# Issuing layer 1's context experts in pieces between the phases of layer 2 that read only latent tokens

## The chip, the cores and the metric

The kernel runs as one program on one core of a Trainium2 chip. The metric is the device time of that program in microseconds (us), lower is better. The kernel before takes 5995.83 us, the median of three runs (5993.45 to 5997.48).

## The reference

Two layers of one block run over 512 latent tokens and 256 context tokens, width 1024. Everything is float32. Per layer, cut to what matters here:

```python
mod_lat = cond_lat @ w_mod[l] + b_mod[l]          # and mod_ctx, from another condition
h  = rmsnorm(x) * (1 + sc1) + sh1;  hc = the same of ctx
p  = h @ w_in[l]                                   # q, k, v | short conv | hyena | gates
kvc = hc @ w_in[l][:, K0:SC0]                      # all the last layer needs of the context
y_att = attend(q, [kc, k], [vc, v])                # latent queries see context keys and values
y_sc, y_hy = short_conv(...), hyena(...)           # hyena: FFT convolutions with generated filters
x = x + gt1 * merge(gates, y_att, y_sc, y_hy)      # and ctx likewise, in layer 1 only
h2 = rmsnorm(x) * (1 + sc2) + sh2                  # and h2c
f = peer(h2 and h2c): per token and each of 8 heads
      s1, s2 = top16 of 128 scores each; top16 of their 256 sums -> 16 expert numbers e, softmax g
      a = gelu(u_tab[e] . h2);  f = sum(g * a * v_tab[e])
x = x + gt2 * f[latent];  ctx = ctx + gt2c * f[context]
```

Two layers run. The context is updated in layer 1 and read in layer 2 by the keys and values of attention alone, so everything of layer 2 that comes from x alone, up to attention, needs no context experts.

## The kernel before, in words

Tokens lie in tiles of 128 on the partitions: 4 latent tiles (NT_LAT), 2 context tiles. The program is a chain of phases. A `Phase` is a block with one instruction stream for each engine; all engines meet at its end. No scheduler orders anything: each engine runs its stream as written and waits on semaphores.

Per layer the phases are: `phase_mod` (24 blocks of w_mod of 1 MB, each split into a rounded high part and a low part, products on TensorE; the filter network's angles on GpSimd), `phase_norm1`, `phase_qkv`, `phase_attention`, `phase_conv_branches` (24 column blocks of w_in, each 24 matmuls per 512 tokens), then `phase_spectrum` and `phase_long_conv` for each of two orders (and for each length, 512 and 256, in layer 1), `phase_merge`, `phase_out`, `phase_norm2`, `phase_query`, `phase_experts`.

`SplitRing` feeds the weight blocks: SyncE loads block n into slot n % slots once the job that used the slot is done, ScalarE rounds it (L296), GpSimd subtracts (L262), TensorE uses it. In `phase_conv_branches` the ring has 4 slots.

`phase_experts` (L1686) is a loop over tiles (6 in layer 1, 4 in layer 2), heads (8) and 16 experts per head. One expert of one head and tile is one item; 768 items in layer 1, of which 256 are of the context. For an item GpSimd issues an indirect DMA of one row of 8 KB (u and v) for each of 128 tokens into one of 8 slots (L1733); VectorE forms the dot product (L1837); ScalarE takes Gelu (L1767); VectorE scales an identity by it (L1845); TensorE multiplies that diagonal by the v half, two float32 matmuls of 512 columns that the profile shows as four rows (L1749). The slot is then free. Between the items of a head VectorE finds the next head's 16 experts in five parts.

Of the kernel before, what the change touches and what calls it, by code (L numbers as in the profile page):

```python
# [138 lines left out]
class Phase:  # L139
# [4 lines left out]
    def __init__(self, nc):  # L144
        self.nc, self.sems = nc, []
        Phase.count += 1
        self.tag = f"p{Phase.count}"
# [6 lines left out]
    def __enter__(self):  # L154
        self.stack = ExitStack()
        self.block = self.stack.enter_context(self.nc.Block())
        return self
# [8 lines left out]
class Chip:  # L166


    def __init__(self, nc, ctx, io):
        self.nc, self.io = nc, io  # L170
        self.arena_at, self.views = (nc.sbuf_base + 31) // 32 * 32, {}
        self.arena = ctx.enter_context(nc.sbuf_tensor("arena", [P, 201 * 256], F32))
# [160 lines left out]
def filter_hidden(c):  # L333

    return c.at(107, T_ALL)


class FilterMlp:


    def __init__(self, c, ph, layer, width):
        self.c, self.layer, self.width = c, layer, width
        self.z, self.h1, self.h2 = c.at(160, T_ALL), c.at(163, T_ALL), filter_hidden(c)
        self.a, self.r = c.at(166, 2, T_ALL), c.at(172, T_ALL)
        self.w1, self.w2 = c.at(176, FH), c.at(176.25, FH)
# [3 lines left out]
    def sync(self, sp):  # L349
        io, layer = self.c.io, self.layer  # L350
        sp.dma_start(self.z[0:EMB, :], io["feat"]).then_inc(self.landed, 16)
# [16 lines left out]
    def vector(self, dve, i):  # L368
# [4 lines left out]
        c.nc.vector.tensor_scalar(self.a[0:FH, i, 0:self.width], c.psum[0:FH, at:at + self.width], c.cols[0:FH, b:b + 1],  # L373
                                  c.cols[0:FH, b + 1:b + 2], ALU.add, ALU.mult).then_inc(self.shifted, 1)

    def gpsimd(self, pool):

        nc, st = self.c.nc, Steps(pool, self.steps)
        r, w = self.r[0:FH, 0:self.width], slice(0, self.width)
        for i in range(2):  # L380
            a, part = self.a[0:FH, i, w], self.z[0:FH, w]
            pool.wait_ge(self.shifted, i + 1)
            if i:
                pool.wait_ge(self.sined, 1)
            st.do(nc.gpsimd.tensor_scalar(r, a, 1.0 / TWO_PI, ROUND, ALU.mult, ALU.add))
            st.wait()
            st.do(nc.gpsimd.tensor_scalar(r, r, ROUND, None, ALU.subtract))
            st.wait()
            for piece in (PI_HI, PI_MID, PI_LO):
                st.do(nc.gpsimd.tensor_scalar(part, r, piece, None, ALU.mult))  # L390
                st.wait()
                st.do(nc.gpsimd.tensor_tensor(a, a, part, ALU.subtract))
                st.wait()
            nc.gpsimd.tensor_scalar(r, a, PI_F32, -PI_F32, ALU.min, ALU.max).then_inc(self.reduced, 1)

    def scalar(self, act, i):
        act.wait_ge(self.reduced, i + 1)
        self.c.nc.scalar.activation((self.h1, self.h2)[i][0:FH, 0:self.width], self.r[0:FH, 0:self.width],
                                    ACT.Sin).then_inc(self.sined, 1)


def phase_mod(c, layer, full):
# [18 lines left out]
    with Phase(nc) as ph:  # L421
# [4 lines left out]
        mlp = FilterMlp(c, ph, layer, T_ALL if full else L_LAT)  # L426
# [17 lines left out]
        def _(act):  # L444
# [6 lines left out]
            for n in range(2 * chunks):  # L451
# [17 lines left out]
                if n in (12, 23):  # L469
                    mlp.scalar(act, n // 23)  # L470
# [3 lines left out]
        def _(pool):  # L474
            mlp.gpsimd(pool)
# [31 lines left out]
        def _(dve):  # L507
# [21 lines left out]
            for t in range(NT):  # L529
# [3 lines left out]
                c.mod[:], c.psum[:, 7 * 512:7 * 512 + 2 * N_MOD].rearrange("p (j s) -> p j s", s=2),  # L533
                c.cols[:, C_BMOD:C_BMOD + N_MOD].unsqueeze(2).to_broadcast([P, N_MOD, 2]), ALU.add))
# [96 lines left out]
def phase_qkv(c, layer, full):  # L631

    nc, io = c.nc, c.io
    qT, kT, vN = c.at(116, PAIRS, T_ALL), c.at(128, KV_HEADS, T_ALL), c.at(134, NT, P)
    sqb = c.at(143, 2, 640)
    qn = c.at(148, 2, 640)
    qr = c.at(153, 2, 640)
    kd = c.at(158, 2, 256)
    tmp = c.at(160, 4, 320)
    gain = c.at(166, 640)  # L640
    w = c.rounded(72, 6, KD, P), c.rounded(48, 6, KD, P)
    ssq = c.at(169, 2, 16)
    rr = c.at(169.5, 2, 16)
    tiles = list(range(NT))
    with Phase(nc) as ph:
# [14 lines left out]
        def _(pe):  # L660
            def project(t):
# [4 lines left out]
                pairs = products((c.hT_high, c.hT_low), w)  # L666
# [582 lines left out]
def phase_long_conv(c, length, order):  # L1249

    nc = c.nc
# [743 lines left out]
```

## Time and profile before

| | us |
|---|---|
| median of 3 runs | 5995.83 |
| profiled execution, span from first to last instruction | 6004.9 |
| layer 1's expert loop, 6 tiles | 2105.0 |
| layer 2's expert loop, 4 tiles | 1412.0 |
| layer 2, from the end of layer 1's loop to the start of `phase_merge` | 661.5 |

The profiled execution and the runs without a profile differ by 0.2%. A row of the profile's page gives an engine's busy time in the span; a stretch of time (a "window") can be asked for its busy times, TensorE's granted clock (1.00 is 2.4 GHz, 0.50 is 1.2 GHz) and the share of time in which the 16 DMA engines were busy. The two expert loops take 59% of the span. TensorE is busy 78% of the span, VectorE 62%, ScalarE 21%, GpSimd 32%, and 1342 of 1503 MB are moved by the gathers.

### The profile page before, as it was taken

The numbers are of one execution on the slowest core, as the hardware profiler recorded it, in microseconds if no ns is written. First come the engines' busy times: TensorE is split into PE (matmuls) and PEld (weight loads), VectorE is DVE, ScalarE is ACT, GpSimd is POOL, SyncE is SP. The second block draws the span as 40 slices with busy tenths as digits, with TensorE's granted clock in tenths as the row PEclk, the third lists the DMA queues.
The fourth block names the chain that finished last, engine by engine and source line by source line (L and its number), as shares of the span: only waits on it lengthen the run. The fifth ranks groups of instructions, "written<-read, shape, count | busy, mean of one in ns | idle before, by whom it ended". The sixth has DMA issues, their size and how long they took to land. (4 is left out here: it accounts for less than half of the span.)

```text
span 6004.9 us, 54671 instructions
## 1 busy us (share of the span) xinstructions
PE 4691.4 (78%) x14264; PEld 2532.4 (42%) x14264; DVE 3701.3 (62%) x8357; ACT 1237.8 (21%) x2616; POOL 1943.0 (32%) x1532
## 2 busy tenths in 40 slices
PE   6999879977777777777777777998977777777776
PEld 3567348855232323222333325563864223233322
DVE  6422451343777778777877876234234778778777
ACT  5322012212111111111111134320322111111111
POOL 4012002222443434444343432120432333444443
PEclk8899989979898889888888887999988889888888
DMA  5011002204999999999999981020314999999998
GB/s 215 15 35 68 4 26 64 67 28 168 386 394 383 384 385 396 383 380 397 378 387 379 400 356 43 28 74 7 98 69 195 380 394 381 385 382 396 381 384 343
DMA packets 223038, 1503.36 MB, mean 250 GB/s; under 512 B 25284, under 2 KB 25668, under 8 KB 51852
## 3 DMA queue, kind: packets, MB, share of 16 engines
q0 software_dynamic: 184320, 1342.26, 55.2%
q1 hardware_dynamic: 38412, 157.98, 7.3%
q8 instruction: 75, 1.23, 0.1%
q14 instruction: 231, 1.89, 0.1%
HBM read 1498.04 MB, written 2.10 MB: 250 GB/s over the span
## 5 line engine op out<-in xcount | busy, mean ns | idle before, releaser
L1749 PE MATMUL psum<-arena 128*128 128x512 f32 x5120 | 2554.1, 656 | 960.4 <-DVE arena L1845 955.3
L1733 POOL DMA_INDIRECT arena<-in_uv,arena x1280 | 1415.0, 1105 | 2072.4 <-PE psum L1749 1715.3
L1749 PEld LDWEIGHTS psum<-arena 128*128 128x128 f32 x5120 | 1040.9, 210 | 2472.8 <-DVE arena L1845 1368.8
L1837 DVE SCALAR_TENSOR_TENSOR arena<-arena 128x1024 f32<-128x1024 f32 x1280 | 1555.3, 1220 | 254.1 <-issue 194.1
L947 PE MATMUL psum<-view_at,view_at 128*128 128x512 f32 (+1 forms) x4896 | 949.6, 356 | 19.2 <-issue 9.7
L262 POOL TENSOR_TENSOR view_at<-view_at,view_at 128x1024 fp32r<-128x1024 f32 (+1 forms) x184 | 396.5, 2166 | 1490.3 <-ACT view_at L296 1489.0
L947 PEld LDWEIGHTS psum<-view_at,view_at 128*128 128x128 f32 x4896 | 812.8, 190 | 153.1 <-issue 21.7
L1767 ACT ACTIVATE arena<-arena 128x1 f32<-128x1 f32 x1280 | 252.2, 202 | 2932.7 <-DVE arena L1837 2930.6
L1845 DVE TENSOR_SCALAR arena<-ident,arena 128x128 f32<-128x128 f32 x1280 | 451.3, 353 | 57.4 <-ACT arena L1767 49.2
L1482 DVE TENSOR_TENSOR view_at<-view_at,psum 128x768 f32<-128x768 f32 (+1 forms) x48 | 39.4, 821 | 372.0 <-PE psum L947 372.0
L1871 DVE TENSOR_TENSOR arena<-psum,arena 128x1024 f32<-128x1024 f32 x80 | 98.0, 1225 | 267.8 <-PE psum L1749 267.8
L262 DVE TENSOR_TENSOR view_at<-view_at,view_at 128x2048 fp32r<-128x2048 f32 (+5 forms) x122 | 200.5, 1670 | 72.9 <-ACT view_at L455 44.0
L296 ACT ACTIVATE view_at<-view_at 128x1024 fp32r<-128x1024 f32 (+1 forms) x172 | 159.6, 938 | 386.5 <-DMA view_at<-in_w_in 255.5
L874 DVE TENSOR_REDUCE arena<-psum 128x1 f32<-128x768 f32 (+1 forms) x80 | 68.1, 851 | 172.8 <-PE psum L834 172.2
L1767 ACT ACT_TABLE_LOAD x120 | 154.0, 1283 | 11.3 <-issue 9.8
L495 PE MATMUL psum<-view_at,cond 128*4 128x512 f32 x384 | 108.7, 424 | 48.3 <-ACT view_at L455 25.1
L1532 PE MATMUL psum<-view_at,view_at 128*128 128x512 f32 x480 | 115.4, 403 | 30.8 <-POOL view_at L262 17.3
L1191 PE MATMUL psum<-arena 128*128 128x512 f32 x288 | 126.2, 594 | 4.2 <-DVE arena L1229 4.2
L670 PE MATMUL psum<-view_at,view_at 128*128 128x256 f32 (+1 forms) x528 | 97.9, 349 | 29.4 <-PEq L163 29.4
L1796 DVE COPY arena<-arena 128x256 f32 (+1 forms) x82 | 23.5, 286 | 157.5 <-POOL arena L1721 157.5
L1532 PEld LDWEIGHTS psum<-view_at,view_at 128*128 128x128 f32 x480 | 93.7, 196 | 52.1 <-issue 29.6
L1790 DVE MAX8 arena<-arena 128x8 f32<-128x128 f32 (+1 forms) x246 | 83.5, 339 | 37.6 <-DVE arena L1788 36.1
(187 smaller groups left out, 3778.5 us busy)
## 6 DMA issues: line engine op xcount, KB each, us to landing
view_at<-in_w_in SPq DMA_DIRECT2D x108, 512.0 KB, 5.1
view_at<-in_w_mod SPq DMA_DIRECT2D x48, 1024.0 KB, 11.3
arena<-in_uv,arena POOLq DMA_INDIRECT x1280
view_at<-in_w_br SPq DMA_DIRECT2D x48, 256.0 KB
arena<-in_dft SPq DMA_DIRECT2D x2, 4096.0 KB
view_at<-in_w_out SPq DMA_DIRECT2D x16, 512.0 KB, 8.6
view_at<-in_wq SPq DMA_DIRECT2D x16, 512.0 KB
arena<-in_x SPq DMA_DIRECT2D x1, 2048.0 KB
```

What stands on the lines that cost most here:

```text
L262: return eng.tensor_tensor(lo, x, hi.bitcast(F32), ALU.subtract)
L296: self._high(act, lambda out, x: self.c.nc.scalar.activation(out, x, ACT.Copy), n)
L495: last = nc.tensor.matmul(c.bank(q % 2, 512, 4), c.cond4[:, half * HALF + k], part[:, n % 2, k * 512:(k + 1) * 512], start=(half == 0 and ...
L947: last = nc.tensor.matmul(c.psum[:, bank * 512 + lo:bank * 512 + hi], a[:, k], b[:, k, lo:hi], start=(k == 0 and i == 0), stop=(k == kt - ...
L1191: last = nc.tensor.matmul(out, table, hw[:, t, src * W_BR:(src + 1) * W_BR], start=(i == 0), stop=(i == nt - 1))
L1532: last = nc.tensor.matmul(c.bank(2 * (t % 4) + h), a[:, k, t * P:(t + 1) * P], b[:, 4 * h:4 * h + 4, k, :], start=(k == 0 and i == 0), sto ...
L1733: nc.gpsimd.indirect_dma_start(out=slots[k % RING], out_offset=None, in_=table, in_offset=bass.IndirectOffsetOnAxis(ap=eidx[:, p, k:k + 1] ...
L1749: last = nc.tensor.matmul(c.bank(2 * p + h), diag[:, k % 4], slots[k % RING][:, D + h * 512:D + (h + 1) * 512], start=(k == 0), stop=(k == ...
L1767: nc.scalar.activation(gelus[:, p, k:k + 1], dots[:, p, k:k + 1], ACT.Gelu).then_inc(gelued, 1)
L1837: nc.vector.scalar_tensor_tensor(out=junk[:, k % 2], in0=slots[k % RING][:, 0:D], scalar=1.0, in1=h2N[:, bass.ds(t, 1)].rearrange("p a n - ...
L1845: nc.vector.tensor_scalar(diag[:, k % 4], c.ident[:], gelus[:, p, k:k + 1], probs[:, p, k:k + 1], ALU.mult, ALU.mult).then_inc(diag_ready, 1)
L1871: nc.vector.tensor_tensor(upd, c.psum[:, 1024 * p:1024 * p + D], gate2[:, bass.ds(t // NT_LAT, 1)].rearrange("p a n -> p (a n)"), ALU.mult ...
```

## The change

Layer 1's `phase_experts` now runs over the 4 latent tiles only. The 256 items of the context are written out without a loop by a class `CtxExperts`, whose four methods issue the items of one engine up to a given number. A `Share` tells a phase how many items stand behind each of its steps. Layer 2 starts with `context_beside`: modulation (24 steps, 48 items), latent spectra (13 steps and 40 items each), norm of the latent tokens (9 steps, 12), convolution projections (24 steps, 88), the two long convolutions (7 steps, 12; 9 steps, 16). Behind them stand a norm phase for the context alone, then qkv, attention, merge as before.

An item differs in this: 6 slots for gathers and not 8, Gelu and the diagonal both on ScalarE (three instructions L495, L499, L504 of the new kernel), the sums of all 8 heads of a tile stay in one pair of PSUM banks. Each engine issues the items up to another bound: GpSimd 3 ahead of the step's number, VectorE to it, ScalarE 1 and TensorE 2 behind it.

```diff
+class CtxExperts:
+    RING, SUM_LAG, FETCH = 6, 2, 3
+    def gather(self, pool, n):
+        for i in range(self.n_gathered, self.up_to(n, self.FETCH)):
+            if i >= self.RING:
+                pool.wait_ge(self.slot_used, i - self.RING + 1)
+            nc.gpsimd.indirect_dma_start(...)
+    def weigh(self, act, n):
+        for i in range(self.n_weighed, self.up_to(n, -1)):
+            act.wait_ge(self.dotted, i + 1)
+            nc.scalar.activation(gelus, dots, ACT.Gelu)
+            nc.scalar.activation(scaled, gelus, ACT.Copy, scale=probs)
+            if i >= 4:
+                act.wait_ge(self.slot_used, i - 3)
+            nc.scalar.activation(self.diag[:, i % 4], self.c.ident[:], ACT.Copy, scale=scaled)
+    def sum_up(self, pe, n):
+        for i in range(self.n_summed, self.up_to(n, -self.SUM_LAG)):
+            pe.wait_ge(self.diag_ready, i + 1)
+            for h in range(2): nc.tensor.matmul(self.c.bank(6 + h), ...)
+    def dot(self, dve, n):
+        for i in range(self.n_dotted, n):
+            dve.wait_ge(self.landed[i % self.RING], 16 * (i // self.RING + 1))
+            nc.vector.scalar_tensor_tensor(out=self.junk, in0=slot, in1=h2N, accum_out=dots)
+class Share:
+    def place(self, s):
+        return self.first + self.n * (s + 1) // self.steps
+def phase_mod_beside(c, layer, lay, share):   # as phase_mod, 3 slots, low parts by DVE (even) and GpSimd (odd)
+            for n in range(n_all):             # GpSimd's stream
+                if n % 2:
+                    split(nc, nc.gpsimd, high, low, raw)
+                next(angles, None)             # one piece of the filter's angles
+                share.gpsimd(pool, n)
 def phase_conv_branches(...):
-        ring = SplitRing(c, ph, conv_blocks(c, layer), ahead=4)
+        ring = SplitRing(c, ph, conv_blocks(c, layer), at=lay.ring_at, slots=lay.ring_slots, ahead=lay.ahead)
...   # in layer 2 ring_slots = ahead = 3
+            for n in range(len(jobs)):         # GpSimd's stream
+                if n + lay.ring_slots < len(jobs):
+                    ring.split(pool, blocks=(n + lay.ring_slots,))
+                share.gpsimd(pool, n)
                 feature_job(c, ring.parts(n), ...).then_inc(proj, 1)      # TensorE's stream
...
+                share.tensor(pe, n)
                 ring.round_ahead(act, n, proj)                            # ScalarE's stream
...
+                share.scalar(act, n)
+                share.vector(dve, n)                                      # VectorE's stream
+def context_beside(c, layer, lay):
+    phase_mod_beside(c, nxt, lay, Share(experts, 0, 48, 24))
+    for order in range(2):
+        phase_spectrum(c, nxt, L_LAT, order, lay, Share(experts, 48 + 40 * order, 88 + 40 * order, 13), spectra[order])
+    phase_norm1_apart(c, range(NT_LAT), ..., Share(experts, 128, 140, KD + 1), [(keep_x, x_lat)])
+    phase_conv_branches(c, nxt, lay, Share(experts, 140, 228, 24), [(keep_ysc, lay.ysc)])
+    for order, (first, last) in enumerate(((228, 240), (240, 256))):
+        phase_long_conv(c, L_LAT, order, lay, Share(experts, first, last, 7 + 2 * order), loads of the kept spectra)
+    phase_norm1_apart(c, range(NT_LAT, NT), ..., Share(), [(x_lat, keep_x), (lay.ys[1], keep_ysc)])
```

Since the gather slots and the context's scores hold memory that layer 2 used, the latent x, the short convolution's result and both spectra are stored to HBM and loaded back. The blocks of phases with items close without GpSimd's drain.

ScalarE's stream in layer 2's `phase_conv_branches` before: L1054 evacuates a job's product, L296 rounds weight blocks, L1059 prepares the convolution.

```order
L1054 ACTIVATE arena<-psum 128x512
L296 ACTIVATE view_at_1527<-view_at_1525 128x1024
L1059 ACTIVATE arena<-arena,cols 128x512
L296 ACTIVATE view_at_1527<-view_at_1525 128x1024 x2
L1054 ACTIVATE arena<-psum 128x512
L296 ACTIVATE view_at_1527<-view_at_1525 128x1024
```

The same place now: L1570 and L1575 are the old L1054 and L1059, L297 the rounding, L495, L499 and L504 an item's Gelu, weight and diagonal, L486 the softmax of the next head.

```order
L1570 ACTIVATE arena<-psum 128x512
L297 ACTIVATE view_at_14342<-view_at_14340 128x1024
L495 ACTIVATE arena<-arena 128x1
L499 ACTIVATE arena<-arena 128x1
L504 ACTIVATE arena<-ident,arena 128x128
L495 ACTIVATE arena<-arena 128x1
L499 ACTIVATE arena<-arena 128x1
L504 ACTIVATE arena<-ident,arena 128x128
L486 ACT_TABLE_LOAD
L486 ACTIVATE arena<-arena 128x16
L495 ACT_TABLE_LOAD
```

The items of a step stand behind the rounding of the block that comes three jobs later.

GpSimd's stream in the same phase before: L262 makes the low parts, L997 restores h at the end.

```order
L999 UNCONDITIONAL_BRANCH
L262 TENSOR_TENSOR view_at_1526<-view_at_1525,view_at_1527 128x1024 x20
L997 TENSOR_TENSOR view_at_49<-view_at_50,view_at_51 128x768 x3
```

The same place now: L263 is the old L262 and L475 the gather of an item.

```order
L1509 UNCONDITIONAL_BRANCH
L263 TENSOR_TENSOR view_at_14341<-view_at_14340,view_at_14342 128x1024
L475 DMA arena<-in_uv,arena 128x2048 x3
L263 TENSOR_TENSOR view_at_14341<-view_at_14340,view_at_14342 128x1024
L475 DMA arena<-in_uv,arena 128x2048 x4
L263 TENSOR_TENSOR view_at_14341<-view_at_14340,view_at_14342 128x1024
L475 DMA arena<-in_uv,arena 128x2048 x4
```

The three or four gathers of a step stand behind the low part of the block three jobs later, and the restoring of h is gone in layer 2.

GpSimd's stream in layer 2's modulation now (before it held only the filter's angles): L697 to L707 are pieces of these angles.

```order
L907 UNCONDITIONAL_BRANCH
L475 DMA arena<-in_uv,arena 128x2048 x5
L263 TENSOR_TENSOR view_at_10729<-view_at_10726,view_at_10732 128x2048
L475 DMA arena<-in_uv,arena 128x2048 x4
L263 TENSOR_TENSOR view_at_10728<-view_at_10725,view_at_10731 128x2048
L697 TENSOR_SCALAR arena<-arena 64x512
L475 DMA arena<-in_uv,arena 128x2048 x2
L700 TENSOR_SCALAR arena<-arena 64x512
L475 DMA arena<-in_uv,arena 128x2048 x2
```

Between every second pair of gathers GpSimd now makes the low part of a block of 2048 columns, which VectorE made before.

## Rows read from the trace of the kernel before

**Rows 1.** The page: span and busy time of each engine.

```profile
span 6004.9 us, 54671 instructions
PE 4691.4 (78%) x14264; PEld 2532.4 (42%) x14264; DVE 3701.3 (62%) x8357; ACT 1237.8 (21%) x2616; POOL 1943.0 (32%) x1532
```

**Rows 2.** Windows of the two expert loops, layer 1 then layer 2.

```profile
core 0: us, PE busy (x) PEld busy (x) DVE busy (x) ACT busy (x) POOL busy (x), PEclk, DMA share, GB/s
1434.40:3539.40 2105.00, 1530.59 (x3072) 624.73 (x3072) 1659.69 (x4262) 326.15 (x987) 849.72 (x769) 0.87 0.95 383
4577.50:5989.50 1412.00, 1023.53 (x2048) 416.20 (x2048) 1112.90 (x2854) 218.04 (x659) 565.57 (x513) 0.87 0.94 381
```

**Rows 3.** Groups of instructions in layer 1's loop, by line.

```profile
L1749 PE MATMUL psum<-arena 128*128 128x512 f32 x3072 | 1530.6, 655 | 573.1 <-DVE arena L1845 569.6
L1837 DVE SCALAR_TENSOR_TENSOR arena<-arena 128x1024 f32<-128x1024 f32 x768 | 933.1, 1220 | 149.0 <-issue 112.8 <-DMA arena<-in_uv,arena 33.3
L1733 POOL DMA_INDIRECT arena<-in_uv,arena x768 | 849.6, 1106 | 1240.3 <-PE psum L1749 1023.1 <-issue 154.2 <-DVE arena L1824 63.1
L1767 ACT ACTIVATE arena<-arena 128x1 f32<-128x1 f32 x768 | 151.3, 202 | 1757.4 <-DVE arena L1837 1756.9
L1767 ACT ACT_TABLE_LOAD x72 | 92.4, 1283 | 6.8 <-issue 6.0
```

**Rows 4.** Timeline of TensorE in layer 1's loop, around one idle time.

```profile
2399.68 5.31 PE L1749 MATMUL psum<-arena 128*128 128x512 f32 x12
...
2415.03 10.89 PE L1749 MATMUL psum<-arena 128*128 128x512 f32 x20 [10.04 <-DVE arena L1845]
```

**Rows 5.** Windows of layer 2's phases: modulation, norm, conv branches, (spectrum, long conv) twice.

```profile
3539.40:3627.30 87.90, 65.54 (x292) 25.86 (x292) 65.12 (x41) 62.41 (x54) 46.47 (x18) 0.92 0.71 289
3627.30:3656.50 29.20, 8.61 (x48) 7.22 (x48) 25.74 (x34) 13.71 (x22) 10.26 (x4) 0.62 0.29 109
3856.30:4000.50 144.20, 134.81 (x608) 111.22 (x608) 36.68 (x45) 42.20 (x56) 54.04 (x23) 0.98 0.23 73
4000.50:4059.40 58.90, 55.35 (x118) 22.97 (x118) 20.75 (x24) 7.41 (x9) 0.00 (x0) 0.86 0.22 81
4059.40:4100.50 41.10, 30.80 (x72) 13.55 (x72) 22.17 (x34) 1.19 (x2) 0.00 (x0) 0.96 0.00 0
4100.50:4159.10 58.60, 53.74 (x118) 21.78 (x118) 20.74 (x24) 7.41 (x9) 0.00 (x0) 0.88 0.04 9
4159.10:4200.60 41.50, 32.15 (x104) 21.15 (x104) 22.88 (x42) 1.54 (x4) 0.00 (x0) 0.92 0.00 1
sum 461.40, PE 380.99 PEld 223.75 DVE 214.07 ACT 135.88 POOL 110.77; mean PE 54.43 PEld 31.96 DVE 30.58 ACT 19.41 POOL 15.82
```

**Rows 6.** Timeline of layer 2's conv branches: jobs, then one block's way.

```profile
3904.62 30.76 PE L947 MATMUL psum<-view_at,view_at 128*128 128x512 f32 x135
...
3933.38 0.78 ACT L1070 ACTIVATE arena<-psum,cols 128x512 f32<-128x512 f32 x1 [0.86 <-PE psum L947]
...
3936.96 1.06 ACT L296 ACTIVATE view_at<-view_at 128x1024 fp32r<-128x1024 f32 x1 [2.80 <-DMA view_at<-in_w_in]
3937.92 0.40 ACT L1044 ACTIVATE arena<-arena 128x256 f32<-128x256 f32 x1
3938.10 2.40 POOL L262 TENSOR_TENSOR view_at<-view_at,view_at 128x1024 fp32r<-128x1024 f32 x1 [3.11 <-ACT view_at L296]
```

**Rows 7.** Groups in layer 2's modulation: the split by VectorE, the rounding, the angles.

```profile
L262 DVE TENSOR_TENSOR view_at<-view_at,view_at 128x2048 fp32r<-128x2048 f32 x24 | 58.0, 2429 | 21.4 <-ACT view_at L455 21.3
L455 ACT ACTIVATE view_at<-view_at 128x2048 fp32r<-128x2048 f32 x24 | 45.8, 1908 | 28.4 <-DMA view_at<-in_w_mod 14.4 <-PE psum L495 13.9
L390 POOL TENSOR_SCALAR arena<-arena 64x512 f32<-64x512 f32 x6 | 18.7, 3111 | 0.5
L385 POOL TENSOR_SCALAR arena<-arena 64x512 f32<-64x512 f32 x2 | 1.2, 616 | 47.7 <-DVE arena L373 47.7
```

**Rows 8.** Timeline of layer 2's norm: a subtraction on VectorE alone, then beside GpSimd's.

```profile
3630.36 0.69 DVE L262 TENSOR_TENSOR view_at<-view_at,view_at 128x512 fp32r<-128x512 f32 x1 [0.24 <-ACT view_at L600]
...
3633.58 5.11 POOL L262 TENSOR_TENSOR view_at<-view_at,view_at 128x1024 fp32r<-128x1024 f32 x2 [13.57 <-ACT view_at L296]
3634.05 2.43 DVE L262 TENSOR_TENSOR view_at<-view_at,view_at 128x512 fp32r<-128x512 f32 x1 [1.50 <-ACT view_at L600]
```

More of the change, by code:

```diff
@@ L386, in gpsimd @@
             st.wait()
-            st.do(nc.gpsimd.tensor_scalar(r, r, ROUND, None, ALU.subtract))
+            yield
+            st.do(nc.gpsimd.tensor_tensor(a, a, part, ALU.subtract))
             st.wait()
[L389 to L394, printed above, removed]
@@ L474, in _ @@
         def _(pool):
-            mlp.gpsimd(pool)
+            for i in range(2):
+                for _ in mlp.gpsimd(pool, i):
+                    pass
         @ph.block.tensor
@@ L811, in phase_attention @@
             "values_summed", "y_kept", "dve_steps"))
-        ring = SplitRing(c, ph, conv_blocks(c, layer)[:4])
+        ring = SplitRing(c, ph, conv_blocks(c, layer)[:0 if lay.apart else lay.ahead])
         @ph.block.sync
@@ L992, in _ @@
             ring.load(sp, proj)
+            if stores:
+                sp.wait_ge(sc_done, KB_BR)
+                for dst, src in stores:
+                    sp.dma_start(dst, src).then_inc(stored, 16)
+                sp.wait_ge(stored, 16 * len(stores))
         def restore(eng, ks):
@@ L1000, in _ @@
         def _(pool):
-            ring.split(pool)
-            pool.wait_ge(proj, len(jobs))
-            restore(nc.gpsimd, range(5, KD))
+            ring.split(pool, blocks=range(lay.ahead, lay.ring_slots))
+            for n in range(len(jobs)):
+                if n + lay.ring_slots < len(jobs):
+                    ring.split(pool, blocks=(n + lay.ring_slots,))
+                share.gpsimd(pool, n)
+            if not lay.apart:
+                pool.wait_ge(proj, len(jobs))
+                restore(nc.gpsimd, range(5, KD))
         @ph.block.tensor
@@ L1115, in dft_views, with phase_spectrum @@
         at += tiles * w / 256
-    out["all"] = c.at(48, int((at - 48) * 256))
+    out["all"] = c.at(first, int((at - first) * 256))
     return out
-def spectrum_views(c, nt):
-    return c.at(152, nt, W_BR), c.at(160, nt, W_BR), c.at(168, W_BR)
 def spectrum_jobs(nt):
     return [(w, f) for f in range(nt) for w in ("re", "im")] + [("top", 0)]
-def phase_spectrum(c, layer, length, order):
+def phase_spectrum(c, layer, length, order, lay, share, keep=None):
     nc, io = c.nc, c.io
@@ L1154, in _ @@
             if order == 0:
-                sp.dma_start(tab["all"], io[f"dft{length}"]).then_inc(tab_in, 16)
+                sp.dma_start(*lay.filter_tables(io, length)).then_inc(tab_in, 16)
+            if keep is not None:
+                for n, (what, ft) in enumerate(jobs):
+                    sp.wait_ge(kept, n + 1)
+                    src, to = {"re": (kre[:, ft], ft), "im": (kim[:, ft], nt + ft), "top": (kre_b, 2 * nt)}[what]
+                    sp.dma_start(keep[:, to], src).then_inc(stored, 16)
+                sp.wait_ge(stored, 16 * len(jobs))
         @ph.block.tensor
@@ L1206, in _ @@
                 nc.scalar.activation(ab[t % 2], hw[:, t], ACT.Abs).then_inc(ab_d, 1)
+                share.scalar(act, t)
+            for n in range(len(jobs)):
+                share.scalar(act, nt + n)
+        @ph.block.gpsimd
+        def _(pool):
+            for n in range(nt + len(jobs)):
+                share.gpsimd(pool, n)
         @ph.block.vector
```

732 lines of the change are left out of this document (602 added, 130 removed).

## The prediction

> **What bounds the kernel now.** I read the page first, then windows of both expert loops and of layer 2's phases, then the groups by line inside them, and last timelines where a wait decides. The page gives the weights: TensorE is busy 78% of 6004.9 us, VectorE 62%, ScalarE 21% [rows 1]. The windows say that two regimes alternate. In an expert loop the DMA engines are busy 94 to 95% at 381 to 383 GB/s while TensorE is idle 27% of the time [rows 2]. Layer 1's loop takes 2105.0 / 768 = 2.741 us for an item, and its 1.049 MB at 383 GB/s take 2.738 us, so the transfer alone fills the time. In the phases the reverse holds: the conv branches keep TensorE busy 135 of 144 us with the DMA engines at 23%, the spectra 55 of 59 us at 4 to 22%, and only the modulation loads the DMA engines to 71% [rows 5]. Work for idle engines therefore exists on both sides. What decides is how four streams that run strictly in order pass each other.
>
> **What leaves.** The loop of 6 tiles becomes one of 4. Layer 2's loop is such a loop, 1412.0 us [rows 2]; 2105.0 - 1412.0 = 693.0 us leave. The seven phases that get items in exchange took 461.4 us [rows 5]. A norm for the context alone is added outside. The nearest row is the norm of all tokens, 29.2 us; its matmuls are a third, but it rounds the same six weight blocks and reloads 3 MB, so I take 27 us (bounds 20 and 33). Attention, qkv and merge are left at their price: merge loses a rounding of h of some 4 us at its start and waits for its first block instead, so nothing. The break-even length of the mixed stretch is 693.0 + 461.4 - 27 = 1127 us. Whatever it takes less is gained.
>
> **What an item costs in the mixed stretch.** TensorE: four rows. Twelve rows take 5.31 us at the full clock, 0.443 us each, 1.77 us an item [rows 4]; the loop's mean is 1530.6 / 3072 = 0.498, 1.99 us an item, at a granted clock of 0.87 [rows 2, 3]. DMA: 2.7 us. VectorE: 1.30 us for the dot, and of the loop's 1659.7 / 48 = 34.6 us for a head some 6 for the search, so 1.7 us. ScalarE: three dependent instructions of about 0.2, 0.2 and 0.3 us with their waits, 1.0 us (no row shows the chain; bounds 0.7 and 1.5), and twice a table load of 1.28 us for each head [rows 3], where Gelu and the softmax alternate.
>
> **Floors.** The DMA engines must move 268 MB of gathers, 42 MB of weights and tables for these phases and some 12 MB of stores and reloads: 322 MB at 383 GB/s is 841 us. TensorE has 381 us of its own [rows 5] and 256 x 1.77 = 453: 834 us. No order goes below about 850 us, so the gain can't pass 280 us. The rest is order, phase by phase.
>
> **Modulation, 24 steps, 2 items each.** Two steps move 2 x 1.05 + 4 x 1.05 = 6.3 MB, 16.4 us. GpSimd's stream is as long: of two steps' four gathers the last of the even step waits for the slot that TensorE frees with its first sum, then the odd block's subtraction follows, twice 2.4 = 4.8 us (a 1024-column one takes 2.40 [rows 6]), and TensorE's low products and the next step (3.5 us of sums, 2.7 of its own) close the circle: about 17 us. In the trace an operation of GpSimd waits for VectorE's: the angle operations of 0.62 us take 3.11 us while VectorE splits [rows 7]. I add 1 us: 18 x 12 = 216, plus 16 for the first search, gather and weight block, plus 4 at the end: 236 us (bounds 205 and 265).
>
> **Spectra, 13 steps, 40 items each.** TensorE is busy 94% already, so items add in full: 58.9 + 40 x 1.77 = 130, plus 2 us because the last piece of the spectrum is stored before the phase closes: 132 each, 264 (bounds 250 and 295). The DMA engines need 117 us of the 132, and six slots must turn in 6 / 3.08 x 9.3 = 18 us, which is enough but not by much.
>
> **Latent norm.** Its chain of squares, root and scaling now stands in the open: 12 us, then 8 steps of 4.4 us of VectorE with 1.3 items each, 3 at the end: 50 us (bounds 43 and 60).
>
> **Conv branches, 24 steps, 3.67 items each: the term that decides.** A job takes 24 x 30.76 / 135 = 5.47 us [rows 6]. If sums only followed jobs, a step would be 5.47 + 3.67 x 1.77 = 12.0 us and the phase some 295. But with 3 slots the load of block n+3 may start only when job n is done, and ScalarE's stream has the rounding of that block ahead of the step's Gelus. In the trace the evacuation after a job starts at 3933.38 and the wait for the block ends at 3936.96, 3.6 us later; the rounding takes 1.06 [rows 6]. Before, ScalarE stood there for nothing that TensorE waited for. Now TensorE's next job is queued behind its sums, and these behind ScalarE. ScalarE had weighed one item more than TensorE had summed, so after job n TensorE sums one item (1.8 us) and stands until 3.6 + 1.06 + 0.4 for the mirror copy + 1.0 = 6.1 us after the job's end, then sums the other 2.67. With the loop's 1.99 us for an item, since 4 us of idle in each step take the clock down at times (after 10.04 us of idle 20 rows took 10.89 us, 0.54 each [rows 4]), this is 5.47 + 6.1 + 5.3 + 0.4 for table loads + 0.4 for matmuls at half clock = 17.7 us. The last three steps have no load: 12.7. So 21 x 17.7 + 3 x 12.7 + 4 = 414 us (bounds 300, with the wait hidden, and 480, with 3 us more for a load beside gathers).
>
> The trace has no weight load beside a gather, so for this wait it shows only the 3.6 us. The Trainium skill, "DMA: Bandwidth & Descriptors", section on queues, rings and completion order, says that each DMA engine takes turns between its rings, a packet of one and then of the other; then a block of 512 KB beside a full gather queue would need some 1.3 us more, and the phase 27 us more. By GpSimd's order the gathers of a step are issued after the block has landed, so most loads would meet a short queue; I leave the sum by the row.
>
> **Long convs.** The first waits for 4.4 MB of tables and spectrum at its start, 12 us, and its 12 items add 21 us of which 6 lie beside VectorE's products: 41.1 + 27 = 68. The second waits 6 us for 2.4 MB, adds 16 x 1.77 = 28 and drains the last gathers, 4: 79 us. Together 147 (bounds 130 and 170). Phase ends: 6 us.
>
> **Sum.** 236 + 264 + 50 + 414 + 147 + 6 = 1117 us against 1127: 10 us gained on 6004.9, or 0.2%. On the median of 5995.8 that is 5986; I say 5985. So 693 us of loop leave, and nearly the same comes back.
>
> **Rival 1, the streams slide past each other (faster).** If the load's wait is hidden, by ScalarE running a job ahead, or since the ring is refilled sooner than I read it, the conv branches take 300 us, with all else as above 1003: 124 us gained, 5872. For it speaks that DMA and TensorE floors lie at 850. Against it speaks the order of ScalarE's stream, which is fixed, and that ScalarE already waits for a block there, 2.80 us at the one shown [rows 6].
>
> **Rival 2, GpSimd and VectorE shut each other out (slower).** Place: modulation and conv branches. In the trace a VectorE subtraction of two SBUF operands takes 0.69 us alone and 2.43 us where it starts 0.5 us into GpSimd's of 2.55 us [rows 8]: it waits until the other is done. The dot products are of that shape, and 12 subtractions of 4.8 us, 21 of 2.4 us and 18 pieces of angles now stand on GpSimd among 136 dots. If each such meeting delays both and the delay reaches the gathers, a pair of steps in the modulation takes 21 us and not 18 (36 us more), and a conv step 20 us and not 17.7 (48 us more). With 15 us more in the spectra for slots that turn too late, that is 99 - 10 = 89 us lost: 6085. It decides from about 1 us a pair and 0.5 us a step upwards, which would turn the small gain. The Trainium skill, "SBUF — State Buffer", section on the two separate sides, gives this as a rule (one exclusive lock, held for the whole instruction, if VectorE reads two SBUF operands and GpSimd reads SBUF); by that rule, rows 8 agree. Against this rival: VectorE and GpSimd are far from full in the sum, 1.7 us of 4.6 us per item.
>
> **Rival 3, bound by DMA throughout.** The gathers then flow at the loop's rate with the weights between them, 870 to 950 us in all: 5740 to 5820. The slots speak against it, since six slots are held over a job, the wait and three sums.
>
> **How the numbers follow.** My case, about even, 0.45, own range 5940 to 6035 (conv step 16 to 19 us, modulation 225 to 250). Rival 1 0.17, rival 2 0.28, rival 3 0.05, something not seen 0.05, of either sign. A measurement of this kernel tells about 0.2%, 12 us, from no change. Faster by more: half of my case, rivals 1 and 3: 0.46. Within: 0.13. Slower: 0.41. The range of 8 in 10 goes from rival 1 to rival 2: 5870 to 6090.
>
> **What would show it.** In the profile after: layer 1's loop at 1412 us; the mixed stretch near 1117 us; in the conv branches a step of 17 to 18 us, ScalarE's rounding ended by a DMA, and TensorE's second item of a step ended by ScalarE some 6 us after the job. If TensorE's idle there is below 1 us a step, rival 1 holds; if VectorE's dots or GpSimd's subtractions are much longer than 1.22 and 2.4 us, rival 2. A modulation well over 265 us or spectra over 150 us each would break the other terms.

## The result, and the profile after

| | us | lowest to highest |
|---|---|---|
| before, timed again beside the change, 6 runs | 6000.69 | 5993.45 to 6012.40 |
| after, 6 runs | 6033.97 | 6017.56 to 6040.89 |
| after / before | 1.0052 | 95% interval 1.0038 to 1.0067 |

The kernel became slower by 0.5%, where a gain of 0.2% was forecast. The page of the kernel after gives the weights that answer to [rows 1].

```profile
span 6031.2 us, 53598 instructions
PE 4711.4 (78%) x14264; PEld 2550.9 (42%) x14264; DVE 3609.8 (60%) x8032; ACT 1400.4 (23%) x3123; POOL 1985.3 (33%) x1537
```

Between the two profiled executions lie 26 us. TensorE's busy time rose by 20 us and ScalarE's by 163, VectorE's fell by 92; what that means for the time is read stage by stage. The windows of the two expert loops answer to [rows 2]; both run over 4 tiles now.

```profile
core 0: us, PE busy (x) PEld busy (x) DVE busy (x) ACT busy (x) POOL busy (x), PEclk, DMA share, GB/s
1429.80:2868.90 1439.10, 1001.43 (x2048) 410.82 (x2048) 1111.97 (x2854) 217.78 (x659) 548.39 (x513) 0.88 0.92 374
4683.80:6015.60 1331.80, 1024.31 (x2048) 417.61 (x2048) 1108.70 (x2854) 217.64 (x659) 589.91 (x513) 0.89 0.99 403
```

The same code with the same 512 items takes 1439 us in one place and 1332 us in the other, where the forecast had 1412 for both. The windows of the mixed stretch answer to [rows 5]: modulation, two spectra, latent norm, conv branches, two long convolutions, and at the end the norm of the context alone.

```profile
2869.20:3140.50 271.30, 191.97 (x476) 82.59 (x476) 158.15 (x263) 107.33 (x198) 147.50 (x81) 0.73 0.77 290
3140.50:3274.00 133.50, 122.22 (x278) 51.57 (x278) 88.23 (x193) 50.66 (x139) 44.35 (x40) 0.96 0.90 338
3274.00:3408.50 134.50, 122.06 (x268) 51.12 (x269) 87.93 (x194) 48.17 (x131) 43.08 (x37) 0.92 0.85 318
3408.50:3472.00 63.50, 38.83 (x95) 17.09 (x94) 47.46 (x92) 30.07 (x70) 24.63 (x18) 0.84 0.83 325
3472.00:3923.50 451.50, 338.63 (x959) 192.88 (x957) 199.03 (x411) 132.65 (x345) 146.84 (x109) 0.85 0.62 229
3923.50:3998.00 74.50, 50.13 (x109) 21.44 (x110) 38.31 (x77) 11.16 (x34) 12.89 (x11) 0.84 0.60 227
3998.00:4080.00 82.00, 68.15 (x183) 35.67 (x182) 47.23 (x84) 20.06 (x63) 16.64 (x14) 0.92 0.57 214
4080.00:4108.80 28.80, 5.99 (x22) 4.03 (x20) 20.08 (x24) 12.46 (x20) 9.81 (x4) 0.61 0.55 219
```

Laid beside the sum of the forecast (its long convolutions, 68 and 79 us, are one term here):

| term, us | forecast | profile after | adds to the time |
|---|---|---|---|
| leaves layer 1's loop | 693.0 | 665.9 | +27.1 |
| modulation | 236 | 271.3 | +35 |
| both spectra | 264 | 268.0 | +4 |
| latent norm | 50 | 63.5 | +14 |
| conv branches | 414 | 451.5 | +38 |
| both long convolutions | 147 | 156.5 | +10 |
| phase ends (inside the rows above) | 6 | | -6 |
| norm of the context | 27 | 28.8 | +2 |
| layer 2's loop | unchanged | 1412.0 to 1331.8 | -80.2 |
| everything else | unchanged | | -5.8 |

The sum is some +36 us, and takes the forecast of -10 to the +26 of the two profiled executions. Two things have to be explained: 94 us in the mixed stretch, and two loops whose time moved by +27 and -80 although nothing in them was edited.

**The conv branches.** The longest waits of engines in that phase (line, what it waited for, total us, times, longest):

```profile
POOL view_at L263 <- ACT view_at L297: 243.3, 21, 18.7
...
ACT view_at L297 <- DMA view_at<-in_w_in: 112.6, 21, 15.5
PE psum L518 <- ACT arena L504: 111.5, 27, 7.9
```

One step on the timeline, to be read beside [rows 6]:

```profile
3645.02 6.05 PE L1456 MATMUL psum<-view_at,view_at 128*128 128x512 f32 x24
...
3650.91 1.88 PE L518 MATMUL psum<-arena 128*128 128x512 f32 x4
...
3655.48 1.06 ACT L297 ACTIVATE view_at<-view_at 128x1024 fp32r<-128x1024 f32 x1 [3.77 <-DMA view_at<-in_w_in]
...
3656.61 2.34 POOL L263 TENSOR_TENSOR view_at<-view_at,view_at 128x1024 fp32r<-128x1024 f32 x1 [11.00 <-ACT view_at L297]
...
3657.44 3.78 PE L518 MATMUL psum<-arena 128*128 128x512 f32 x4 [4.65 <-ACT arena L504]
...
3659.10 0.96 POOL L475 DMA_INDIRECT arena<-in_uv,arena  x1
```

The job ends at 3650.9, TensorE sums one item, and the second item's sum starts at 3657.44, 6.5 us after the job; the forecast was 6.1. ScalarE's rounding (L297) waits for the block and everything behind it waits with it. The last row shows what the forecast did not name: GpSimd's next gather (L475) is issued only after its subtraction (L263), so it waits for the same rounding.

**The modulation.** Its dot products (L608) and subtractions, where [rows 7] and [rows 8] are the rows of before:

```profile
L608 DVE SCALAR_TENSOR_TENSOR arena<-arena 128x1024 f32<-128x1024 f32 x48 | 84.4, 1757 | 83.5 <-DMA arena<-in_uv,arena 83.3
L940 PE MATMUL psum<-view_at,cond 128*4 128x512 f32 x192 | 70.6, 508 | 81.2 <-POOL view_at L263 49.7 <-ACT view_at L899 31.1 <-DVE view_at L263 0.4
...
L263 POOL TENSOR_TENSOR view_at<-view_at,view_at 128x2048 fp32r<-128x2048 f32 x12 | 55.6, 4632 | 4.0 <-ACT view_at L899 3.7
```

A dot product takes 1757 ns in the mean, against 1220 in the loop [rows 3], and TensorE waits 49.7 us for GpSimd's low parts of 4.63 us each. These waits come once in a pair of steps; the first and the last are

```profile
2906.52 1.87 PE L940 MATMUL psum<-view_at,cond 128*4 128x512 f32 x4 [3.47 <-POOL view_at L263]
...
3128.48 1.87 PE L940 MATMUL psum<-view_at,cond 128*4 128x512 f32 x4 [4.12 <-POOL view_at L263]
```

Eleven pairs in 222.0 us are 20.2 us a pair, where the forecast had 18 and rival 2 had 21.

**The loops.** VectorE's dot products in the two loops of the kernel after, layer 1 then layer 2 (the row for layer 1 answers to [rows 3]):

```profile
L2394 DVE SCALAR_TENSOR_TENSOR arena<-arena 128x1024 f32<-128x1024 f32 x512 | 621.5, 1218 | 95.3 <-issue 72.1 <-DMA arena<-in_uv,arena 21.1
```

```profile
L2394 DVE SCALAR_TENSOR_TENSOR arena<-arena 128x1024 f32<-128x1024 f32 x512 | 621.5, 1218 | 28.5 <-DMA arena<-in_uv,arena 26.6
```

Busy time is equal to a tenth of a microsecond. The idle time "issue", in which VectorE waited for nothing that the profile shows, stands in one loop alone. It lies at one place of each turn of the loop over pairs of heads; the place answers to the 10.04 us of idle in [rows 4]:

```profile
2074.87 1.22 DVE L2394 SCALAR_TENSOR_TENSOR arena<-arena 128x1024 f32<-128x1024 f32 x1 [4.61 <-issue]
...
2079.47 0.08 DVE L2394 DVE_READ_ACCUMULATOR arena<-arena 128x1 f32 x1 [2.23 <-issue]
...
2080.07 2.93 PE L2306 MATMUL psum<-arena 128*128 128x512 f32 x3 [12.32 <-DVE arena L2402]
```

The DMA view of the same two windows has a queue of kind "instruction" (packets, MB, share); each packet is 8192 B. Layer 1's loop, then layer 2's:

```profile
q14 instruction: 79, 0.65, 0.1%
```

```profile
q14 instruction: 5, 0.04, 0.0%
```

79 packets are about 5 for each of the 16 turns. Layer 1's loop has 30 stalls of VectorE of over 1.9 us with no releaser, 100 us in all, and each ends 1.8 to 2.0 us after the start of one of these packets.

### The profile page after: what moved, and what is told of

Read it like the earlier page. It is cut to its first block and busy times, and to the rows that moved or that the text cites. A ratio compares the mean times of both kernels' runs of the same rounds, so it can differ in the third digit from the quotient of the medians.

```text
span 6031.2 us, 53598 instructions
## 1 busy us (share of the span) xinstructions
PE 4711.4 (78%) x14264; PEld 2550.9 (42%) x14264; DVE 3609.8 (60%) x8032; ACT 1400.4 (23%) x3123; POOL 1985.3 (33%) x1537
## 5 line engine op out<-in xcount | busy, mean ns | idle before, releaser
L2306 PE MATMUL psum<-arena 128*128 128x512 f32 x4096 | 2025.7, 651 | 742.7 <-DVE arena L2402 738.9
L2290 POOL DMA_INDIRECT arena<-in_uv,arena x1024 | 1138.0, 1111 | 1601.4 <-PE psum L2306 1317.3
L2394 DVE SCALAR_TENSOR_TENSOR arena<-arena 128x1024 f32<-128x1024 f32 x1024 | 1243.0, 1218 | 123.8 <-issue 72.1
L1456 PE MATMUL psum<-view_at,view_at 128*128 128x512 f32 (+1 forms) x4896 | 965.9, 359 | 17.1 <-PEq L164 8.2
L263 POOL TENSOR_TENSOR view_at<-view_at,view_at 128x1024 fp32r<-128x1024 f32 (+1 forms) x196 | 452.8, 2320 | 1552.0 <-ACT view_at L297 1547.0
L1456 PEld LDWEIGHTS psum<-view_at,view_at 128*128 128x128 f32 x4896 | 816.7, 191 | 163.4 <-issue 32.4
L518 PE MATMUL psum<-arena 128*128 128x512 f32 x1024 | 554.4, 689 | 145.9 <-ACT arena L504 144.2
L608 DVE SCALAR_TENSOR_TENSOR arena<-arena 128x1024 f32<-128x1024 f32 x256 | 353.6, 1381 | 194.0 <-DMA arena<-in_uv,arena 185.8
L475 POOL DMA_INDIRECT arena<-in_uv,arena x256 | 292.0, 1141 | 523.3 <-PE psum L518 403.1
L2402 DVE TENSOR_SCALAR arena<-ident,arena 128x128 f32<-128x128 f32 x1024 | 361.2, 353 | 51.3 <-ACT arena L2324 43.0
L297 ACT ACTIVATE view_at<-view_at 128x1024 fp32r<-128x1024 f32 (+1 forms) x176 | 163.8, 940 | 442.1 <-DMA view_at<-in_w_in 311.8
L263 DVE TENSOR_TENSOR view_at<-view_at,view_at 128x2048 fp32r<-128x2048 f32 (+5 forms) x102 | 165.1, 1641 | 80.1 <-ACT view_at L2004 41.6
L2428 DVE TENSOR_TENSOR arena<-psum,arena 128x1024 f32<-128x1024 f32 x64 | 78.4, 1225 | 212.6 <-PE psum L2306 212.6
L1718 PE MATMUL psum<-arena 128*128 128x512 f32 x288 | 129.6, 596 | 6.1 <-DVE arena L1766 6.0
L940 PE MATMUL psum<-view_at,cond 128*4 128x512 f32 x192 | 70.6, 508 | 81.2 <-POOL view_at L263 49.7
L495 ACT ACTIVATE arena<-arena 128x1 f32<-128x1 f32 x256 | 50.2, 196 | 350.5 <-DVE arena L608 347.6
```

The source lines that it names most:

```text
L263: return eng.tensor_tensor(lo, x, hi.bitcast(F32), ALU.subtract)
L297: self._high(act, lambda out, x: self.c.nc.scalar.activation(out, x, ACT.Copy), n)
L475: nc.gpsimd.indirect_dma_start(out=self.slots[i % self.RING], out_offset=None, in_=self.table, in_offset=bass.IndirectOffsetOnAxis(ap=self ...
L518: last = nc.tensor.matmul(self.c.bank(6 + h), self.diag[:, i % 4], self.slots[i % self.RING][:, D + h * 512:D + (h + 1) * 512], start=(j = ...
L608: nc.vector.scalar_tensor_tensor(out=self.junk, in0=self.slots[i % self.RING][:, 0:D], scalar=1.0, in1=self.h2N[:, u // PH], op0=ALU.mult, ...
L1456: last = nc.tensor.matmul(c.psum[:, at + lo:at + hi], a[:, k], b[:, k, lo:hi], start=(k == 0 and i == 0), stop=(k == kt - 1 and i == 2))
```

## The experiments

Two questions were put to the chip. For the loops: does VectorE's loop code pay for where it lies in VectorE's instruction stream? For the mixed stretch: which order of which stream holds the conv step and the modulation pair?

**Moving the loop's code in the kernel before.** The edit puts instructions that do nothing for the computation (increments of a semaphore that nobody waits for) ahead of layer 1's loop on VectorE. Layer 2's loop lies behind them in the same program and moves by as many instructions.

```diff
+        padded = ph.sem("padded")
...
+            if layer == 0:
+                for _ in range(32):     # 64 and 96 in the next two
+                    dve.sem_inc(padded, 1)
             dve.sem_inc(psum_used, 2)
```

> The kernel before with 32 more semaphore increments on VectorE ahead of layer 1's expert loop, nothing else. Theory P (place of the loop's code): in both profiles an expert loop that fetches 8 KB blocks of instructions in every turn (119 in layer 1's and 78 in layer 2's of before, 79 in layer 1's of after) has VectorE idle for 2 to 5 us a turn with no releaser and takes 2.74 to 2.81 us an item; the one with 5 fetches in all (layer 2's of after) takes 2.60. If the place decides, one of the shifts of 32, 64, 96 instructions brings a loop to about 2.60 us an item: layer 1's loop from 2105 to about 2000 us, or layer 2's from 1412 to about 1332. Rival M (memory: the tables' addresses or the new HBM tensors set the gather rate): all loops stay at 2.74 to 2.76 us, total 5996 to 6005.

> As the shift by 32, by 64 instructions. Theory P: at least one loop of the three shifts at 2.60 us an item, and fetches in it near none. Rival M: no loop moves by over 1%.

> As the shift by 32, by 96 instructions. Theory P: at least one loop of the three shifts at 2.60 us an item, and fetches in it near none. Rival M: no loop moves by over 1%.

| instructions added | median us | ratio to before, interval | loop 1, loop 2, us | instruction packets in the loops |
|---|---|---|---|---|
| 0 | 5997.59 | 1 | 2105.0, 1412.0 | 119, 78 |
| 32 | 5806.79 | 0.9686 (0.9668 to 0.9703) | 1991.2, 1330.8 | 4, 3 |
| 64 | 5806.78 | 0.9688 (0.9671 to 0.9704) | 1995.4, 1327.9 | 4, 3 |
| 96 | 5992.15 | 0.9991 (0.9981 to 1.0001) | 2106.4, 1403.7 | 120, 78 |

(The loops and packets of the first line are those of the profile before.) The windows of both loops with 32 added show that the gathers then run at 404 GB/s where they ran at 383 [rows 2]:

```profile
1426.90:3418.10 1991.20, 1509.78 (x3072) 618.46 (x3072) 1657.58 (x4262) 325.94 (x987) 860.27 (x769) 0.90 0.99 404
4459.50:5790.30 1330.80, 1006.87 (x2048) 412.01 (x2048) 1109.68 (x2854) 218.12 (x659) 567.38 (x513) 0.91 0.98 403
```

32 instructions that do nothing take 191 us out, 64 as many, and 96 nothing: position decides, not the number. With this the prediction's reading of the loop falls too: it took 383 GB/s for what the transfer can do.

**The same on ScalarE**, as a control for a change of timing at the loop's start.

```diff
+            if layer == 0:
+                for _ in range(32):
+                    act.sem_inc(padded, 1)
             softmax_exp(0, 0)
```

> A control: the kernel before with 32 semaphore increments on ScalarE (not VectorE) ahead of layer 1's loop. If VectorE's place alone decides, both loops keep their 2.74 to 2.76 us an item and the total stays at 5997; if any delay or shift at the loop's start does it, it falls to 5807.

5996.09 us, ratio 0.9999 (0.9990 to 1.0009), 120 and 79 packets. It is VectorE's stream that counts.

**Two positions between**, one run each, so without an interval: 16 and 80 added.

> The kernel before with 16 increments on VectorE: its loops start at instructions 986 and 1981. 982 was bad in the changed kernel, 1002 good here. It narrows the border: layer 1's loop either 2105 or about 1993 us; layer 2's, 16 short of the good 1997, either 1412 or 1331.

> The kernel before with 80 increments on VectorE: loops at 1050 and 2045. 1034 was good, 1066 bad; 2029 good, 2061 bad. If the good places form one stretch per 128 instructions, each loop is either wholly good (2.60 us an item) or wholly bad (2.74), none between.

With 16 the kernel took 6058.21 us, worse than before: layer 1's loop 2211.3 us with 119 packets, layer 2's 1357.5 with 18. With 80 it took 5858.92 us: 2024.7 us with 29 packets and 1348.4 with 17. So a position is not wholly good or wholly bad, as the expectation for 80 had it. In the records of the kernel with 80 the packets of layer 1's loop come about 5 a tile, where the kernel before has 5 in each of the 4 turns of a tile. With 16 the count is that of before, but VectorE stalls twice in a turn and not once. Its idle time ahead of a dot product in layer 1's loop, in the kernel before, with 16 and with 80:

```profile
DVE arena L1837 <- issue: 112.8, 24, 5.6
```

```profile
DVE arena L1838 <- issue: 221.0, 23, 10.0
```

```profile
DVE arena L1838 <- issue: 32.8, 9, 6.5
```

VectorE's stalls of over 1.9 us with no releaser, each of which ends 1.8 to 2.0 us after the start of a packet, account for nearly all of what these loops take more than well placed ones (1991.2 us for 768 items, 1335.2 for 512 in the run a_pad32 below):

| layer 1's loop | stalls | us in all | longer than well placed, us |
|---|---|---|---|
| before | 23 | 103 | 113.8 |
| after | 30 | 100 | 103.9 |
| before, 16 added | 46 | 213 | 220.1 |
| before, 80 added | 5 | 29 | 33.5 |

The windows of the kernels with 16 and with 80, layer 1's loop of each:

```profile
1432.80:3644.10 2211.30, 1516.64 (x3072) 620.15 (x3072) 1659.88 (x4262) 325.99 (x987) 854.64 (x769) 0.86 0.90 365
```

```profile
1426.80:3451.50 2024.70, 1517.86 (x3072) 621.75 (x3072) 1658.18 (x4262) 325.56 (x987) 854.21 (x769) 0.89 0.97 398
```

**The same in the kernel after**, to compare both kernels with both loops well placed. The edit is that of 32 added on VectorE.

> The changed kernel with 32 semaphore increments on VectorE ahead of layer 1's expert loop. Theory P (place of the loop's code): its loop starts at VectorE's instruction 982, before's at 970; before's was cured at 1002 and 1034 and not at 1066. At 1014 it should be cured: layer 1's loop from 1439 to about 1330 us, layer 2's stays at 1332, total 6034 to about 5925. The mixed stretch stays at 1209 us. Rival: the changed kernel's loop is slow for another reason (semaphores, the closed block ahead of it) and stays at 1439.

5927.20 us, ratio to before 0.9882 (0.9865 to 0.9898); loops 1335.2 and 1329.0 us, 4 and 5 packets; mixed stretch 1205.3 us. Divided by the 0.9686 of the kernel before with 32 added, that is 1.0202, with the two intervals taken together about 0.0025 either way. The change proper costs 2.0%, some 120 us, and not 0.5%. Most of that is a smaller removal and a longer stretch: of well placed loops 1991.2 - 1335.2 = 656.0 us leave, the mixed stretch and the context's norm take 1205 + 29, and 656.0 + 461.4 are 117 less than these.

**ScalarE's order in the conv branches.** The items of a step are put ahead of the rounding.

```diff
-                ring.round_ahead(act, n, proj)
                 while rounds < len(turns) and turns[rounds] <= n - 1:
...
                 share.scalar(act, n)
+                ring.round_ahead(act, n, proj)
```

> The changed kernel with one edit: in the conv branches ScalarE issues a step's Gelus and diagonals ahead of the rounding of the block three jobs later, not behind it. Theory S (TensorE's sums stand behind ScalarE's wait for the weight block): TensorE's 111 us of waits for the diagonal in this phase go to under 25, the step falls from 18.8 to some 13 us and the phase from 451 to 315-330 us, total about 5905. Rival D (gathers are late): the waits move to the DMA, the phase stays above 410 us, total above 5990. Rival G (GpSimd and VectorE shut each other out): phase above 400 us.

6032.87 us, ratio 1.0069 (1.0048 to 1.0090) to before: nothing gained over the 1.0052 of the kernel after, where some 130 us were expected. From the end of the latent norm to the phase's last instruction it takes 460.6 us, against 457.5 in the kernel after. The waits moved to the gathers:

```profile
POOL view_at L263 <- ACT view_at L297: 274.9, 21, 20.2
...
DVE arena L608 <- DMA arena<-in_uv,arena: 206.1, 52, 12.6
...
PE psum L518 <- ACT arena L504: 109.8, 48, 8.1
```

VectorE's waits for a gather rose from 94.0 us in 23 to 206.1 in 52. The later rounding makes GpSimd's subtraction later, and the gathers behind it.

**GpSimd's order alone.** Gathers ahead of the subtraction, ScalarE as in the kernel after.

```diff
             for n in range(len(jobs)):
+                share.gpsimd(pool, n)
                 if n + lay.ring_slots < len(jobs):
                     ring.split(pool, blocks=(n + lay.ring_slots,))
-                share.gpsimd(pool, n)
```

> The changed kernel with one edit in the conv branches: GpSimd issues a step's gathers ahead of the subtraction for the block three jobs later. ScalarE's order stays. If the wait for the weight block on ScalarE alone sets the step (my forecast's theory), nothing moves: phase 440-455 us, TensorE still waits for diagonals 5 us a step. If late gathers set it, the phase falls below 400 us.

6032.15 us, 1.0066 (1.0050 to 1.0083); 456.7 us for the phase. ScalarE's wait for the block (115.0 us) and TensorE's for ScalarE (109.1 us in 27) stand as before.

**Both.**

> Both edits in the conv branches: ScalarE's items ahead of the rounding, and GpSimd's gathers ahead of the subtraction. With the first edit alone the phase stayed at 448 us, and VectorE's wait for gathers rose from 94 to 206 us. Theory T (two streams hold the same step: take one wait away and the other ends last): together the phase falls to 320-345 us, total about 5920. If the DMA queue or the six slots limit it, it stays above 400 us.

5899.29 us, 0.9840 (0.9823 to 0.9856); the phase takes 329.3 us, 128 less. Its waits:

```profile
POOL arena L475 <- PE psum L518: 126.1, 49, 6.8
...
POOL view_at L263 <- ACT view_at L297: 27.1, 16, 3.1
...
PE psum L518 <- ACT arena L504: 24.7, 31, 2.0
```

TensorE's wait falls from 111.5 to 24.7 us, and the window of the phase shows TensorE busy 302 of 329 us with the granted clock at 0.99, which was 0.85 in the kernel after:

```profile
3463.70:3793.00 329.30, 301.81 (x964) 176.84 (x964) 192.82 (x416) 137.01 (x351) 160.29 (x110) 0.99 0.87 319
```

A row of an item's sum takes 167.5 / 352 = 0.476 us there, and 0.584 in the kernel after. Each swap alone gives nothing, both give 128 us: two streams held the same step.

**The modulation's low parts, all on VectorE**, as in the kernel before.

```diff
             for n in range(n_all):             # GpSimd
-                if n % 2:
-                    pool.wait_ge(hi_ready, n + 1)
-                    split(nc, nc.gpsimd, high[n % SLOTS], low[n % SLOTS], raw[n % SLOTS]).then_inc(low_pool, 1)
...
             for n in range(n_all):             # VectorE
-                if n % 2 == 0:
-                    dve.wait_ge(hi_ready, n + 1)
-                    split(nc, nc.vector, high[n % SLOTS], low[n % SLOTS], raw[n % SLOTS]).then_inc(low_dve, 1)
+                dve.wait_ge(hi_ready, n + 1)
+                split(nc, nc.vector, high[n % SLOTS], low[n % SLOTS], raw[n % SLOTS]).then_inc(low_dve, 1)
```

> The changed kernel, but VectorE makes all 24 low parts of the modulation and GpSimd none. Theory G (GpSimd's subtractions and VectorE's dots shut each other out, and the gathers queue behind them): the modulation falls from 271 to 225-240 us, the dots there from 1.76 to below 1.4 us. Theory F (a floor of DMA and slots): it stays within 10 us of 271. VectorE's stream is 12 to 24 instructions longer ahead of layer 2's loop, which should stay at 1332.

5980.75 us, 0.9972 (0.9961 to 0.9983). The modulation takes 228 us, 43 less; a pair of steps takes 16.9 us and not 20.2. Its dot products:

```profile
L608 DVE SCALAR_TENSOR_TENSOR arena<-arena 128x1024 f32<-128x1024 f32 x48 | 60.5, 1261 | 41.7 <-DMA arena<-in_uv,arena 41.3
L263 DVE TENSOR_TENSOR view_at<-view_at,view_at 128x2048 fp32r<-128x2048 f32 x24 | 56.8, 2366 | 22.6 <-ACT view_at L899 22.4
```

They are back at 1261 ns although VectorE now makes twice as many subtractions. The Trainium skill, "SBUF — State Buffer", section on the two separate sides, has a VectorE instruction with two SBUF inputs shut out for the whole of a GpSimd instruction that reads SBUF and started first; the dot products have two such inputs, and the 1757 and 1261 ns agree. How much of the 43 us is this lock, and how much that the gathers no longer stand behind 55.6 us of subtractions on GpSimd, the run doesn't part.

**All that helped, together**: both swaps, the modulation's split on VectorE, and 32 instructions ahead of layer 1's loop.

> The changed kernel with all edits that helped: ScalarE's items ahead of the rounding and GpSimd's gathers ahead of the subtraction in the conv branches, all low parts of the modulation on VectorE, and 32 increments on VectorE ahead of layer 1's loop. If the gains add (134 us, 53 us and 107 us off 6033), 5740 us, 1.1% below the kernel before with the increments alone (5807). If the two places of gain share a limit (DMA, slots), 5760 to 5800.

5748.72 us (5735.50 to 5756.70), ratio to before 0.9578 (0.9565 to 0.9591): faster than both kernels. Modulation, conv branches and the two loops in its profile take 221.8, 330.4, 1335.4 and 1328.6 us. Against the kernel before with its loops well placed the quotient is 0.9578 / 0.9686 = 0.9888, about 0.0022 either way: with the streams reordered the change is worth 1.1%.

## Why the prediction was wrong, step by step

- **"Layer 2's loop is such a loop, 1412.0 us; 693.0 us leave": the first step that failed.** It took the loop's price for a property of the loop. It is one of its place: 2.741 and 2.758 us an item before, 2.811 and 2.601 after, 2.593 where the whole loop has 4 instruction packets. The two loops were thereby misjudged by +27 and -80 us. [Rows 4] had the sign of it, 10.04 us of TensorE idle ended by VectorE, and [rows 3] had 112.8 us of VectorE idle put down to "issue"; the prediction took neither as a cost that could go away.
- **"Its 1.049 MB at 383 GB/s take 2.738 us, so the transfer alone fills the time": wrong.** The argument was circular, since 383 was the mean over the stalls. Well placed, the same gathers run at 404 GB/s at a DMA share of 0.99.
- **The conv step, 414: ScalarE's wait right, GpSimd's stream missed, 38 us too small.** The second item's sum 6.5 us after the job (forecast 6.1), ScalarE's rounding ended by a DMA, and a step of 451.5 / 24 = 18.8 us (forecast 17 to 18) are as foretold. TensorE's idle in the window is 451.5 - 338.6 = 112.9 us, where 21 x 4.3 and 4 at the end, 94, were forecast. It is busy 338.6 us, where the forecast's jobs and sums add up to 302: a row of the sums took 0.584 us at a granted clock of 0.85 and not 0.498, and the jobs took 140.2 us for 131. For such things 0.8 us in each of 21 steps, 17 us, had been set aside. 19 + 36 - 17 = 38 us is what the term was short. The prediction let ScalarE alone decide, and this is the step that failed here; a_swap, which removes just that, gained nothing, because GpSimd's stream stood there too.
- **Modulation 236: too small by 35 us, mostly at the place that rival 2 named.** "I add 1 us" stood for the meetings of VectorE and GpSimd in a pair, 18 us in all; a pair took 20.2. That is 26 of the 35 us, and start and end took 29 us for 20. With the low parts on VectorE a pair takes 16.9 us, 3.3 less; rival 2 had 3 us a pair over the 18, 36 us. The 3.3 us need not be the lock alone, since the run also takes GpSimd's subtractions out of the gathers' way. The sign that the prediction read in [rows 7], 0.62 us against 3.11, compares two different lines of the angles and so shows no wait by itself; [rows 8] does.
- **Rival 2 in the conv branches: not the cause.** The dots there took 1377 ns and the subtractions 2.50 us, close to alone, and the 38 us lie in the order of the streams.
- **Rival 1** did not come about by itself. With both swaps the phase takes 329 us, where the rival had 300, and the kernel 98 us less than before, where it had 124; but some 90 of the 98 us are the places of the loops, which cost 195 us before (114 and 81) and 105 with the swaps.
- **Spectra, context norm and what was left at its price: right** (268 for 264, 28.8 for 27; qkv, attention and all from merge to layer 2's loop took 575.0 us after 576.7). The latent norm was 14 us and the long convolutions 10 us too low; no run looked into them.
- **The direction** hung on a gain of 10 us between terms that were wrong by 94, 27 and 80. The mixed stretch turned the sign, by the conv step's second stream and the modulation's pairs above all; the loops hid most of it. Had both loops taken what was forecast, the kernel would have lost some 80 us. The change in itself costs 120 us; the plain comparison shows 33, since layer 2's loop happened to move to a good place. That the measured time lies so near the forecast is luck.

Open: which positions are good. Of the places tried, counted in the built programs, VectorE's loop starting at instruction 1002, 1014, 1034, 1997, 2029, 3125 or 3157 of its program is good; at 970, 982, 986, 1066, 1965 or 2061 it is bad; at 1050, 1981 and 2045 between. That the stalls are fetches of loop code is inferred from the packets, which come and go with them, and from the control on ScalarE; no row names an instruction packet's content.

## What to carry to other kernels

Before an edit near a hardware loop is judged, look at the "instruction" packets and the idle time "issue" inside it in both kernels; if they differ, compare both with the loop's code well placed, since a shift of VectorE's program alone was worth 3% here, more than the change itself in either order of its streams. Where work is slipped between the steps of an in-order pipeline, list every stream in which it stands behind the wait for the slowest input: moving it ahead in one of them gave nothing, in both 128 us. And a rate measured over a stretch with stalls is no floor for the transfer.

## What the runs showed of the hardware that was not expected

- A loop's time can depend on where its code lies in VectorE's program. With about 5 instruction packets of 8192 B in each turn of the inner loop VectorE stalls once or twice a turn, 4.2 to 5.1 us each in layer 1's loop before and with 16 added; TensorE was idle 10 and 12 us at the two places shown, and the kernel took up to 191 us more. With 16 instructions added, 119 packets cost 106 us more than with none. The Trainium skill, "Runtime: NRT & Kernel Launch", section on instruction fetch mechanics, says that a taken branch whose target isn't in the two pages of code that an engine holds forces a DMA fetch before it goes on. By that rule a loop that doesn't fit as placed pays in every turn; the packets and stalls here agree. That a shift by 16 to 32 instructions decides it is shown by the runs alone.
- The gathers of 8 KB rows by one core run at 402 to 404 GB/s in the well placed loops (383 and 381 in [rows 2]).
